# Eight delta-rule heads: projected inside the split-projection stage and run as a three-head pipeline behind the RWKV stage

## What is computed

```python
u = h @ w_in                                  # 2048 -> per head 4 x 128 columns (q, k, v, z)
qkv = silu(centred_dwconv(u[..., :3 * D_GDN], conv_w))    # 5 taps
q, k = l2norm(q) * 128 ** -0.5, l2norm(k)
decay = exp(tril(g[:, None] - g[None, :]))    # chunks of 64 tokens
lmat = strict_lower((k * beta) @ k.T * decay)
tmat = inverse(eye + lmat)
u, wk = tmat @ (v * beta), tmat @ (k * beta * exp(g))
attn = tril(q @ k.T * decay)
for chunk in chunks:
    v_new = u_i - wk_i @ state
    o_i = q_i @ state + attn_i @ v_new
    state = state * exp(g_last) + k_tail.T @ v_new
y = rmsnorm(o) * silu(z)
```

## Time and profile before

| | us |
|---|---|
| median of 3 runs | 4770.96 (4765.27 to 4775.19) |
| the profiled execution, its own time | 4768.8 |
| span from its first to its last instruction | 4766.9 |

### The profile page before, as it was taken

The page is one execution under the profiler, slowest core; times in us unless marked ns, Lnnn a source line. Parts: engine busy times, 40 slices in busy tenths (PEclk is TensorE's granted clock), DMA queues, the critical chain, the costliest instruction groups (busy, mean ns, idle before and its releaser), DMA issues. The chain is left out here.

```text
span 4766.9 us, 58834 instructions
## 1 busy us (share of the span) xinstructions
PE 3907.7 (82%) x21386; PEld 3079.3 (65%) x21386; DVE 2177.3 (46%) x3882; ACT 1053.5 (22%) x1823; POOL 1251.4 (26%) x706
## 2 busy tenths in 40 slices
PE   7778888888984799997688888888596977887697
PEld 2247556655763688886688878778474755675375
DVE  0354553455357425665454554555402267763202
ACT  1111121112111235554122122122102112220201
POOL 0034425333544000000000000000064644555063
PEclk9889899989987899998799999999798988998899
DMA  7223223221331114442211111111332211112131
GB/s 277 97 81 107 95 61 101 92 90 59 120 93 46 35 63 142 138 132 93 72 33 46 35 46 36 34 45 33 113 118 90 86 53 57 62 62 66 53 111 70
DMA packets 256743, 386.60 MB, mean 81 GB/s; under 512 B 142577, under 2 KB 174849, under 8 KB 252097
## 3 DMA queue, kind: packets, MB, share of 16 engines
q1 hardware_dynamic: 243728, 360.14, 24.1%
q10 hardware_dynamic: 12848, 24.24, 1.4%
HBM read 337.43 MB, written 49.50 MB: 81 GB/s over the span
## 5 line engine op out<-in xcount | busy, mean ns | idle before, releaser
L1004 PE MATMUL pjl<-high,w_high 128*128 128x512 f32 x960 | 394.1, 410 | 195.3 <-DVE arena L2602 48.6
L478 PE MATMUL pjl<-hT,ring 128*128 128x512 f32 x1024 | 511.9, 604 | 20.7 <-DMA ring<-in_w_g 12.6
L987 POOL TENSOR_TENSOR w_high<-ring_o,cst 128x1024 fp32r<-128x1024 f32 x152 | 303.4, 1996 | 567.8 <-PE pjl L1006 398.3
L621 POOL TENSOR_TENSOR arena<-arena,RP 128x1024 f32<-128x1024 f32 x128 | 249.2, 1947 | 600.6 <-DMA arena<-in_w_ada 590.1
L1005 PE MATMUL pjl<-low,w_high 128*128 128x512 f32 x960 | 384.2, 400 | 0.0
L1006 PE MATMUL pjl<-high,w_low 128*128 128x512 f32 x960 | 383.1, 399 | 0.0
L989 POOL TENSOR_TENSOR w_low<-ring_o,w_high 128x1024 fp32r<-128x1024 f32 x152 | 377.5, 2484 | 11.9
L1004 PEld LDWEIGHTS pjl<-high,w_high 128*128 128x128 f32 x960 | 187.2, 195 | 251.0 <-issue 166.9
L2128 POOL MEMSET unused<- 128x1 f32 x1 | 0.1, 99 | 1129.1 <-POOLq L187 1129.1
L2592 DVE SCALAR_TENSOR_TENSOR arena<-arena 128x512 f32<-128x512 f32 x232 | 251.8, 1085 | 7.8
L478 PEld LDWEIGHTS pjl<-hT,ring 128*128 128x128 f32 x1024 | 180.3, 195 | 100.4 <-issue 67.9
(11 more groups left out here) (471 smaller groups left out, 8693.6 us busy)
## 6 DMA issues: line engine op xcount, KB each, us to landing
arena<-in_w_ada SPq DMA_DIRECT2D x128, 512.0 KB, 3.9
ring<-in_w_lr SPq DMA_DIRECT2D x72, 512.0 KB, 4.2
arena<-in_w_ada SPq DMA_DIRECT2D x32, 1024.0 KB, 6.8
ring<-in_w_g SPq DMA_DIRECT2D x64, 512.0 KB, 4.4
ring_o<-in_w_out SPq DMA_DIRECT2D x64, 512.0 KB, 3.7
ring_o<-in_w SPq DMA_DIRECT2D x64, 512.0 KB, 3.6
arena_r<-rk_d SPq DMA_DIRECT2D x128, 192.0 KB, 3.5
rk_d<-arena_p SPq DMA_DIRECT2D x72, 192.0 KB, 1.9
```

The costliest lines, as they stand in the source:

```text
L478: last = pe.matmul(lat, ring[:, s, kk % HK], hT[:, kk, 0:LAT], start=kk == 0, stop=kk == KT - 1)
L621: pool.tensor_tensor(w, w, c, ALU.mult).then_inc(S["g_lm"], 1)
L987: pool.tensor_tensor(h, w, one, ALU.mult).then_inc(S[done + "h"], 1)
L1004: pe.matmul(lat, wh[:, c], ah, start=kk == 0, stop=False)
```

## The change

- `phase_gdn` goes behind `phase_rwkv`. The weights of the delta-rule heads are appended to those of the pairs (`w_lr`), `project`, `load_tiles` and the `invert_*` functions go, and `phase_gates` projects nothing; it adds exp of the gates, stored as a third kind of gate rows.
- `phase_proj` has 68 tiles in place of 36: behind the last pair come the four tiles of each of eight heads, by `half_tile` with its three float32r matmuls. Conv, silu, norms and gating of each head are done here, and the results stored to DRAM (`ga_d`, `gv_d`, `gs_d`). The norms are taken as columns, turned into rows, and brought back over DRAM broadcast (`norms_of`). The low parts of the weights stay with VectorE for the first `OWN` = 80 halves (low-rank gates, pairs, head 0); those of heads 1 to 7 are computed by GpSimd.
- The late sums move from `phase_gdn` into this stage. GpSimd now issues the loads itself (`ask`), slice by slice, 256 KB each, into two buffers; VectorE multiplies and adds in one instruction per slice (`later`), 32 slices per head, 256 in all.
- `phase_gdn` is a pipeline of three heads: head m scans, head m+1 inverts, head m+2 starts, on the 18 slots of the scan. Its inversion is the one of the RWKV stage, with three levels of doubling behind the 15 steps.

The core of the diff:

```diff
-PHASES = [(phase_mod, "a"), (phase_gates, "b"), (phase_gdn, "g"), (phase_split, "s"), (phase_proj, "p"), (phase_rwkv, "r"),
+PHASES = [(phase_mod, "a"), (phase_gates, "b"), (phase_split, "s"), (phase_proj, "pq"), (phase_rwkv, "r"), (phase_gdn, "g"),
...
@@ phase_gates
-            for j in range(4):
-                if j:
-                    pe.wait_ge(S["b_raw"], (0, 1, 3, 5)[j])
-                project(pe, e, 0, j, loads(half), pj[0][:, 0:LAT], pj[2][:, 0:CTX] if j in (1, 2) else None)
...
@@ phase_proj, GpSimd
+            def ask(count):
+
+                for _ in range(count):
+                    x = asked[0]
+                    if x < 32 * GH:
+                        if x >= 2:
+                            pool.wait_ge(S["q_lu"], x - 1)
+                        pool.dma_start(late[:, x % 2], io["w_ada"][8 + x // 16, :, x % 16]).then_inc(S[f"q_lw{x % 2}"], 16)
+                        asked[0] += 1
...
+            for h in range(GH - 1):
+                m = OWN + 2 + 8 * h
+                split_low(pool, e, m)
+                split_low(pool, e, m + 1)
+                ask(8)
+                split_low(pool, e, m + 2)
+                split_low(pool, e, m + 3)
+                ask(9)
+                split_low(pool, e, m + 4)
+                ask(5)
+                split_low(pool, e, m + 5)
+                ask(5)
+                if m + 6 < 2 * TILES:
+                    split_low(pool, e, m + 6)
+                ask(5)
+                if m + 7 < 2 * TILES:
+                    split_low(pool, e, m + 7)
+            ask(32)
...
@@ phase_proj, VectorE
+            def later(count):
+
+                for _ in range(count):
+                    x = done[0]
+                    g, k = x // 16, x % 16
+                    which = 0 if g < 4 else 2
+                    c, a = csk[:, 3 * k + which:3 * k + which + 1], acc[:, g % 2]
+                    dve.wait_ge(S[f"q_lw{x % 2}"], x // 2 * 16 + 16)
...
+                        dve.scalar_tensor_tensor(a, late[:, x % 2], c, a, ALU.mult, ALU.add).then_inc(S["q_lu"], 1)
+                    done[0] += 1
...
+            def next_head(h, m, count):
+
+                head_conv(h, 0)
+                later(count)
+                head_silu(h, 0)
+                if h:
+                    weights(m + 6)
+                head_conv(h, 1)
+                later(count)
+                if h:
+                    weights(m + 7)
+                head_silu(h, 1)
+                later(count)
+                weights(m + 8)
+                head_conv(h, 2)
+                dve.wait_ge(S["q_nc"], h + 1)
+                dve.reciprocal(ncol, ncol).then_inc(S["q_rc"], 1)
+                later(count)
+                head_silu(h, 2)
...
+                last.then_inc(S["q_pre"], 1)
+                if h:
+                    keep_share(2 * h - 1)
+                later(8)
+                if more:
+                    weights(m + 4)
+                    weights(m + 5)
+                    later(4)
+                    next_head(h + 1, m, 5)
+                else:
+                    later(24)
+                keep_share(2 * h)
...
@@ phase_proj, TensorE
+                if more:
+                    pe.wait_ge(S["p_ev"], t - 1)
+                    tile(t, 0, False)
+                if h:
+                    share(2 * h - 1)
+                if more:
+                    pe.wait_ge(S["p_ev"], t)
+                    tile(t, 1, True)
+                    pe.wait_ge(S["p_ev"], t + 1)
+                    tile(t, 2, True)
+                    head_norms(h + 1)
+                share(2 * h)
...
@@ phase_gdn, the same on TensorE and ScalarE
+            def fill(m, n):
+
+                if m >= 1:
+                    norm(m - 1, n)
+                if m + 2 < GH:
+                    start(m + 2, n)
+                if m + 1 < GH:
+                    invert(m + 1, n)
```

More of the change, by code:

```diff
@@ L401, in _ @@
             act.activation(y[R], y[R], ACT.Exp, scale=-1.0).then_inc(S["b_y"], 1)
[L402 to L407, removed]
+            for d in range(2):
+                act.wait_ge(S["b_scan"], d + 1)
+                act.activation(eg[d][R], gs[d][R], ACT.Exp).then_inc(S["b_ex"], 1)
+            act.wait_ge(S["b_ex"], 2)
         @block.vector
@@ L468, in _ @@
             dve.wait_ge(S["b_gc"], 6)
[L471 to L482, removed]
@@ L485, in load_tiles @@
[L485 to L523, removed]
@@ new lines, in scan @@
+                    if j >= 2:
+                        if j > 2:
+                            pe.wait_ge(S["g_o"], m * 8 + 2 * (j - 2))
+                        elif m:
+                            pe.wait_ge(S["g_rt"], m)
+                        for d in range(2):
+                            u = G_ORDER[d][j]
+                            pe.matmul(o_[:, d], old[:, d], QG[m % 2][:, d, u * P:u * P + P], start=True, stop=False)
+                            last = pe.matmul(o_[:, d], SA[:, d], MT[m % 3][:, d, u], start=False, stop=True)
+                        last.then_inc(S["g_oo"], 1)
@@ L961, in stream @@
+                    fill(m, 3 * j + 2)
+            dve.memset(eps[:], 1e-6).then_inc(S["g_v0"], 1)
+            dve.wait_ge(S["g_b16"], 16)
+            for n in range(18):
+                start(0, n)
+            for n in range(18):
+                invert(0, n) if n < 3 else None
+                start(1, n)
+                invert(0, n) if n >= 3 else None
+            for m in range(GH):
+                scan(m)
+            for n in range(4, 6):
+                norm(GH - 1, n)
 def stream(sp, e, src, half, tiles, start=0):
@@ L1302, in _ @@
             with pe.Fori(0, PAIRS - 1) as i:
-                period(i, True)
-            period(PAIRS - 1, False)
+                period(i, False)
+            period(PAIRS - 1, True)
+            for h in range(GH):
+                head(h)
         @block.scalar
@@ L1439, in _ @@
             for i in range(PAIRS):
-                period(i, i < PAIRS - 1)
+                period(i)
+            for h in range(GH - 1):
+                n = 16 + 8 * (PAIRS + h)
+                weights(n + 2)
+                weights(n + 3)
+                next_head(h + 1, 40 + 4 * h, n, None)
         @block.vector
@@ new lines, in keep_share, with head_conv @@
+            def keep_share(g):
+                dve.wait_ge(S["q_sh"], g + 1)
+                dve.tensor_copy(modx[:, 4 * g:4 * g + 4], shares).then_inc(S["q_mx"], 1)
+            def head_conv(h, j):
+                m = GT if j else LAT
+                dve.wait_ge(S["q_ps"], 3 * h + j + 1)
+                for o in range(1, CONVK):
+                    ins = dve.scalar_tensor_tensor(qkv[:, j, 0:m], raw[:, j, o:o + m], hp(h, 5 * j + o), qkv[:, j, 0:m], ALU.mult, ALU.add)
+                    if o < CONVK - 1:
+                        link(ins)
+                    else:
+                        ins.then_inc(S["q_conv"], 1)
@@ L1504, in period @@
+            def period(i):
                 m = 16 + 8 * i
@@ L1570, in _ @@
             for i in range(PAIRS):
-                period(i, i < PAIRS - 1)
+                period(i)
+            for h in range(GH):
+                head(h)
+            keep_share(2 * GH - 1)
+            assert done[0] == 32 * GH
+            dve.wait_ge(S["q_mx"], 2 * GH)
+            dve.tensor_tensor(gate[:], modx[:, 0:KT], pr("b_ada", 96).rearrange("p (n s) -> p n s", s=2)[:, 32:48, 0], ALU.add).then_inc(S["q_acc"], 1)
+            dve.tensor_tensor(mod2[:], modx[:, KT:64], pr("b_ada2", 48), ALU.add).then_inc(S["q_acc"], 1)
+            dve.wait_ge(S["q_acc"], 2)
             dve.wait_ge(S["p_mix"], 4)
```

1114 lines of the change are left out of this document (648 added, 466 removed).

## The result

The changed kernel takes 4832.88 us in the median (4823.96 to 4838.65, 4 runs), against 4768.69 us before (4765.27 to 4775.19, 4 runs) on the same chip: ratio 1.0131, 95% interval 1.0112 to 1.0151. It is slower, as forecast, and inside the range, but by 64 us where 21 were forecast (4790 against the profiled 4768.8).

The account below looks back on a forecast made before the run. VectorE, waiting for late-sum slices through two buffers, was to bind the heads' projection. Gates 264.5, split and pairs 592, delta rule 558, RWKV onward 2492 and 1.9 outside make 3908.4; plus D of 882: 4790 us, range 4650 to 4896.

Parts of the forecast that it names:

- TensorE's cost of a head: In the projection stage, a head's four tiles take TensorE 59 us with norms and sums' shares.
- the last head's rest: End of the projection stage: the last head's remaining steps and 32 slices on VectorE, 26.4 + 15R us.
- One head period X on VectorE: In the projection stage, VectorE's time per head: X = 54.5 + 13R, 100 us with R = 3.5.
- The round trip R: Late-sum slices: semaphore to GpSimd, issue, transfer, semaphore back; taken as 3.5 us, between 2.5 and 4.8.
- GpSimd's subtractions beside VectorE: In a head's period: allowances of 3, 3 and 1.8 us for subtractions beside VectorE's work or between slice loads.
- a shorter trip: Rival on slice loads: same mechanism but R below 3.3, total 4684 at 2.5 and 4758 at 3.2; chance 0.33.
- break-even: The stretch D, last pair through heads, at 860.4 us equals the old time; R then about 3.3.
- GpSimd is held up: Rival: slice asks wait behind GpSimd's subtractions and both slow each other; R 4.2 to 4.8, total 4864 to 4928; chance 0.13.
- The slices don't bind: Rival in the projection stage: loads land under other work, X is TensorE's 59 us, total 4462; chance 0.04.
- The delta-rule stage: Rival behind RWKV: three heads' chains meet in every slot, 75 us a head, not 62.5; total 4865; chance 0.06.
- check by the RWKV stage: Check on the delta-rule stage's head time: half a pair in RWKV, same pipeline with more scan work, takes about 66 us.
- Gates: Gates stage: projection and most of a 42.67 us wait for it go, about 4 stay; 303 falls to 264.5 us.

Follow-up runs that it names:

- e1: The changed kernel with only the first two slices loaded, all 256 slice operations kept on old data: 4519.68 us, ratio 0.9479 to the kernel before.
- e4: The changed kernel with only the first two slices loaded and nearly every slice operation cut to one column: 4449.75 us, ratio 0.9332 to the kernel before.
- e5: The changed kernel with a third slice buffer, room made by packing the raw tiles closer: 4676.8 us, ratio 0.9806 to the kernel before.
- e2: The changed kernel with VectorE subtracting all low parts of weights, GpSimd only issuing loads: 4800.93 us, ratio 1.0068 to the kernel before.
- e3: e2 with the slices one by one between VectorE's own instructions, still two buffers: 4694.51 us, ratio 0.984 to the kernel before.
- e6: e3 with the third slice buffer of e5: 4582.78 us, ratio 0.9613 to the kernel before.
- e7: e6 with four slices grouped where VectorE waits for the head's stores, and 33 slices a head: 4564.95 us, ratio 0.9577 to the kernel before.

## Why the prediction was wrong in size

- **The mechanism was right**, and shown by e1, e4 and e5: VectorE waits in its own list for slices that come through two buffers; TensorE, which needs 60.4 us a head, does not bind. The new delta-rule stage (553.8 for 558; 61.2 us a head for 62.5, from the gating products' starts at 3031.10 and 3336.99 five heads apart), TensorE's cost of a head and the last head's rest were within 2.5%.
- **The step that failed is "One head period X on VectorE"**, X = 54.5 + 13R = 100; measured 107.25. Its terms beside what the traces show (us a head; a wait that crosses a window's edge makes the measured ones add up to 107.4):

| term of the period | forecast | measured |
|---|---|---|
| VectorE's own work, undisturbed | 48.8 | 43.4 (e2) |
| GpSimd's subtractions, other contention, half clock | 3 + 3 + 1.8 + 3 = 10.8 | 14.0 (the change against e2) |
| idle until a slice lands | 13 x (3.5 - 0.78) = 35.4 | 43.5 |
| idle for ScalarE | 5.0 | 6.5 |

- **The round trip R** was the largest error, 8.1 us a head. It was sized at 3.5, by the median of an undisturbed row. Undisturbed it is 3.3, even shorter, but the mean is 4.1 in the change and 3.9 in e2, since loads beside the head's stores, and beside gate rows and weights, land up to 10.1 us after issue. The forecast did not think of traffic that the head itself makes.
- **GpSimd's subtractions beside VectorE** were sized 3.2 us too small. The price was read from the taps' mean, 1.288 against 1.05 us, a fifth more. That is a mean over many that never met a subtraction; one that does can stand for its whole length. A count of subtractions by their duration, 8 x 2.4 = 19 us a head, would have been the upper bound. And 3 + 1.8 of the forecast's 10.8 were for loads asked late because a subtraction stands ahead of them. That did not happen: in the seven periods a load was issued 0.3 us after VectorE had left its buffer in the mean, in the change as in e2.
- **Luck**: VectorE's own work was sized 5.4 us a head too large, which hid a good part of both errors. With it right, the forecast would have been 94.6 for a period and further off.
- **TensorE** was to be busy for under 60 us of a period. It needs 60.4 without slices (e4), and in the change its matmuls took 68.3 (478.23 / 7), at a granted clock of 0.78.
- **What the size rested on**: 7 x 7.25 = 51 us against a forecast difference of 21. Since 763 and 871 us nearly cancel, an error of 6% in one large term trebles the result; the range of 4650 to 4896 said so, the single number did not.
- **The rivals**: "a shorter trip" fell, R is not below 3.3 in the mean, though the undisturbed trip lies just at the break-even. "GpSimd is held up" came near in numbers, R of 4.1 for 4.2 or more, but not in mechanism: GpSimd's asks were not late and its subtractions not longer; VectorE's instructions were. "The slices don't bind" is excluded by e1 alone. The delta-rule stage costs 61.2 us a head, not 75. (The forecast's check by the RWKV stage is a little off: a step that stands once in each half of a pair, L1981 of before, comes every 68.5 us in the mean, not 66.)
- **Gates**: 7.5 us less than forecast. I had let the stage end at 264; VectorE's copies into `gc` start at 258.26 to 258.84, where before the chain itself ended, and the next stage's first instruction starts at 260.03 (the cut lies 3.1 ahead of it, as in the windows of before). The new stores take no time on the path.

## What to carry to other kernels

Work that an engine fetches through two buffers inside its in-order list costs the whole round trip again for every pair. A third buffer took back 156 us here (e5), other instructions between the pieces 106 (e3 against e2), both together 218 (e6 against e2). Size such a trip by its mean beside the traffic that the new code makes, not by a row without it. Moving a small elementwise job from VectorE to GpSimd can cost VectorE more than the job: here 14.0 us of longer instructions for 9.1 us of subtractions. Count each such instruction, as an upper bound, at its GpSimd duration on VectorE's side. Before filler is regrouped, look what gap the group stands in; it may cover another wait.

## What the runs showed of the hardware

- A load of 256 KB issued by GpSimd took it 0.54 us and landed 3.0 us after the issue began (median); 4.1 in the median of five beside a head's stores, 8.5 for two beside gate rows and a weight half. With three buffers in place of two the median of the seven periods rose from 3.1 to 3.6. SyncE's issues of 512 KB took it 0.33.
- A VectorE product of 0.69 us took 4.52 beside two GpSimd subtractions of 2.4, which were not lengthened. It does not take loads: a slice's operation is 0.94 us in the mean in the change, 0.95 without loads (e1) and 0.75 without GpSimd's subtractions (e2).
- TensorE's granted clock was lower where it was idle more: in the stretch of the seven heads 0.98 with TensorE idle for 2 us of 423 (e4), 0.89 with 73 of 520 (e7), 0.78 with 273 of 751 in the change, where it waited up to 26.8 us at a time. So part of what an idle TensorE costs is paid behind the wait: the same heads' matmuls were busy for 68 us a period in the change (478.23 / 7) and 60 in e4.
